# Matmuls whose result nobody reads, placed ahead of TensorE's waits in a hybrid mixer and expert trunk

## The chip, the cores and the metric

The kernel runs on one core of one Trainium2 chip. A core has five engines that run their own instruction streams and meet at semaphores: TensorE (PE in the rows; PEld is its weight load), VectorE (DVE), ScalarE (ACT), GpSimd (POOL) and SyncE (SP), which here issues all transfers. TensorE reads SBUF and writes PSUM, which has eight banks of 512 float32 columns on 128 partitions. Its clock has two levels, 2.4 GHz and 1.2 GHz; the profile lists what share of full speed was granted in each stretch (1.00 or 0.50).

The metric is the device time of one execution in microseconds (us), taken as the median of several runs.

## The reference, cut to what matters

Two pre-norm layers work on 256 positions of 1024 channels, in float32. Each has an RMS norm, four mixers that read the same normed input (short convolution, state space, gated MLP, pooling), sigmoid gates, an output projection, a second RMS norm and a channel mixer: dense in layer 0, top 2 of 8 experts in layer 1.

```python
for layer in range(DEPTH):
    h = rmsnorm(x, norm1_g[layer])
    proj = h @ w_in[layer]
    ...
    y_b = mamba2_mixer(z, xbc, dt_raw, ...)      # ends in an RMS norm over 4 groups
    ...
    x = x + merged.astype(x.dtype) @ w_out[layer]
    h2 = rmsnorm(x, norm2_g[layer])
    if layer % 2 == 0:
        f = swiglu(h2, ffn_wg[idx], ffn_wu[idx], ffn_wd[idx])
    else:
        f = moe_ffn(h2, router_w[idx], moe_wg[idx], moe_wu[idx], moe_wd[idx])
    x = x + f
return rmsnorm(x, final_g)
```

## The kernel before

**Arithmetic.** Every large product is made of three fast matmuls: each operand is split into a rounded part (`hi`) and the rest (`lo`), and hi·hi, hi·lo and lo·hi are added up in PSUM (`product`, for 256 columns each; the experts use 512 columns). ScalarE makes `weight_hi` (L367, in the experts L386) and VectorE makes `weight_lo` (L634, L667) from each weight unit of 1 MB that SyncE has loaded; a ring of three units stands between them and TensorE.

**Order.** All engines follow an order written out by hand. In each layer `norm_sums` comes first, then `PLAN`, a list of stages with so many weight units behind each, then the rest of the units. The last stages of `PLAN` are the norm of the state-space branch: `y_sq` (VectorE multiplies and squares, GpSimd adds pairs of squares, L1178), `y_sum` (TensorE sums the squares over channels by matmuls with one column of ones), one weight unit, `y_spread` (TensorE spreads the reciprocal roots over the partitions).

**The norms.** `norm_sums(n)` runs for n = 0 (first norm of layer 0, at the start), n = 1 (second norm of layer 0, inside the last output unit) and n = 2 (first norm of layer 1). It waits for the added squares (POOL L1119) and for the squares of the last channels (DVE L641), sums them into one column, waits for a diagonal matrix of the reciprocal roots (ACT L374, then DVE L646 and L648), and spreads it with one matmul of 256 columns. VectorE then writes h (L658) and `h_lo` (L637), ScalarE `h_hi` (L377), in pairs of channel blocks; TensorE goes on with the dense channel mixer (n = 1), or with the stage `dt_row`, full float32 matmuls over h that wait pair by pair (n = 2).

**Entry to the experts.** Transposes of x and the router's matmuls come in turns with the last output units. VectorE then picks the top two (L935 to L947, `sel_done`); TensorE makes two small matmuls that give each token its place; VectorE turns them into the selection matrix (L954 to L960, `pick_done`); `first_gather` selects the tokens of the first expert block by 32 matmuls of 128 columns; ScalarE and VectorE split the result (L516, L982), and the expert's weight products begin with `up`.

The matmuls all go through one helper, so nearly all of them have the line L1211. The tile `ones_r` holds ones, rounded for the fast matmul; before, the state-space stage `seg` reads it.

Of the kernel before, what the change touches and what calls it, by code (L numbers as in the profile page):

```python
# [100 lines left out]
def trunk(nc, x_in, par_in, con_in, fin_in, mix_w, ff_w, moe_w, out):  # L101
# [4 lines left out]
    with ctx:  # L106
# [36 lines left out]
        def bank(b, n=1):  # L143
            return PS[:, b:b + n, :].rearrange("p b n -> p (b n)")

        def tiles(ap, n=SEQ):
            return ap.rearrange("p (t n) -> p t n", n=n)
# [1061 lines left out]
        def _(pe):  # L1209
            def mm(o, a, b_, start, stop, **k):  # L1210
                return nc.tensor.matmul(o, a, b_, start=start, stop=stop, skip_group_check=True, **k)  # L1211

            def product(o, slot, blk, a_hi, a_lo, start, stop):

                w = slice(blk * P, (blk + 1) * P)
                mm(o, hi[:, slot, w], a_hi, start, False)
                mm(o, hi[:, slot, w], a_lo, False, False)
                return mm(o, lo[:, slot, w], a_hi, False, stop)
# [15 lines left out]
            def norm_sums(n):  # L1234

                for k in (0, 1, KT - 2, KT - 1):
                    if k == 0:
                        pe.wait_ge(S["sq_added"], n + 1)  # L1240
                    elif k == KT - 2:
                        pe.wait_ge(S["sq_done"], PAIRS * (n + 1))
                    for t in range(TT):
                        last = mm(bank(4 + t)[:, 0:1], sq[:, k, t * P:(t + 1) * P], C_("ones", 0, 1), k == 0, k == KT - 1)
                last.then_inc(S["norm_sum"], 1)
                pe.wait_ge(S["diag_done"], n + 1)
                mm(bank(7)[:, 0:SEQ], C_("ones"), diag, True, True).then_inc(S["rstd_ps"], 1)

            def early_unit(layer, u):

# [92 lines left out]
            def stage(name, layer):  # L1343
# [16 lines left out]
                elif kind == "xs_T":  # L1360

                    pe.wait_ge(S["conv_done"], XBC_BLOCKS * layer + 8)
                    pe.wait_ge(S["a_sc"], layer + 1)
                    for t in range(TT):
                        for c in range(8):
                            last = nc.tensor.transpose(bank(6 - 2 * t + c // 4)[:, (c % 4) * P:(c % 4 + 1) * P],
                                                       proj[:, XBC + c, t * P:(t + 1) * P], C_("ident"))
                        last.then_inc(S["xs_T"], 1)
                elif kind == "mean":
                    pe.wait_ge(S["gelu_done"], 2 * layer + 1)  # L1370
                    pe.wait_ge(S["xdt_done"], TT * (layer + 1))
                    for k in range(4):
                        last = mm(bank(7)[:, 0:SEQ], C_("ones"), v_[:, k, :], k == 0, k == 3)
                    last.then_inc(S["mean_sum"], 1)
                elif kind == "var":
                    pe.wait_ge(S["dev_sq"], layer + 1)
                    for t in range(TT):
                        for k in range(4):
                            last = mm(bank(7)[:, t:t + 1], v_sq[:, k, t * P:(t + 1) * P], C_("ones", 0, 1), k == 0, k == 3)
                    last.then_inc(S["var_sum"], 1)  # L1380
                elif kind == "ln":
                    pe.wait_ge(S["v_diag"], layer + 1)
                    mm(bank(7)[:, 0:SEQ], C_("ones"), v_diag, True, True).then_inc(S["v_rstd"], 1)
                elif kind == "v_T":
                    pe.wait_ge(S["v_norm"], layer + 1)
                    for t in range(TT):
                        for n in range(4):
                            last = nc.tensor.transpose(bank(4 + t)[:, n * P:(n + 1) * P], v_[:, n, t * P:(t + 1) * P], C_("ident"))
                    last.then_inc(S["v_T"], 1)
                elif kind == "spatial":  # L1390
                    pe.wait_ge(S["v_T_sb"], layer + 1)
                    pe.wait_ge(S["ws_masked"], layer + 1)
                    for n in range(4):
                        for t in range(TT):
                            at = (n % 2) * SEQ + t * P
                            last = mm(bank(6 + n // 2)[:, at:at + P], vT[:, t, n * P:(n + 1) * P], P_("ws", n * P, P), True, True)
                    last.then_inc(S["s_done"], 1)
                elif kind == "pool_out":
                    pe.wait_ge(S["pooled"], 4 * (layer + 1))
                    for n in range(4):  # L1400
                        last = mm(bank(4 + n // 2)[:, (n % 2) * SEQ:(n % 2 + 1) * SEQ], P_("pool_map", n * P, P), pooled[:, n, :], True, True)
                    last.then_inc(S["pool_out"], 1)
                elif kind == "cb":
                    pe.wait_ge(S["conv_done"], XBC_BLOCKS * (layer + 1))
                    if g == 0:
                        pe.wait_ge(S["yc_f"], layer + 1)
                    else:
                        pe.wait_ge(S["cb_done"], GROUPS * layer + 2)
                    for n in (2 * g, 2 * g + 1):
                        b_t, c_t = proj[:, XBC + 8 + n, :], proj[:, XBC + 12 + n, :]  # L1410
                        mm(bank(6 + n % 2)[:, 0:SEQ], b_t[:, 0:P], c_t, True, True)
                        mm(bank(6 + n % 2)[:, SEQ:SEQ + P], b_t[:, P:], c_t[:, P:], True, True).then_inc(S["cb_ps"], 1)
                elif kind == "seg":
                    pe.wait_ge(S["seg_in"], GROUPS * layer + g + 1)
                    pe.wait_ge(S["yd_f"], layer + 1)
                    pe.wait_ge(S["cb_done"], GROUPS * (layer + 1))

                    for n in range(2):
                        for part in range(2):
                            mm(bank(4 + n), after_r[:], flat(seg_in0[part][:, 2 * n:2 * n + 2, :]), part == 0, False)  # L1420
                        for part in range(2):
                            mm(tiles(bank(4 + n))[:, :, P:], ones_r[:], seg_in1[part][:, 2 * n:2 * n + 2, :], False, part == 1)
                    for part in range(2):
                        last = mm(bank(6), after_r[:], flat(seg_in1[part]), part == 0, part == 1)
                    last.then_inc(S["seg_done"], 1)
                elif kind == "y":
                    pe.wait_ge(S["score_done"], GROUPS * layer + g + 1)
                    if layer or g:
                        pe.wait_ge(S["y_done"], GROUPS * layer + g)
                    for n in range(4):  # L1430
                        head = 4 * g + n
                        o = bank(7)[HEAD_DIM * (n % 2):HEAD_DIM * (n % 2 + 1), (n // 2) * SEQ:(n // 2 + 1) * SEQ]
                        heads = slice(head * HEAD_DIM, (head + 1) * HEAD_DIM)
                        mm(o, xdt[:, 0, heads], dec0[:, n, :], True, False)
                        last = mm(o[:, P:], xdt[:, 1, heads], dec1[:, n, :], False, True)
                    last.then_inc(S["y_ps"], 1)
                elif kind == "y_sum":
                    pe.wait_ge(S["yb_sq_added"], layer + 1)
                    for n in range(GROUPS):
                        for t in range(TT):  # L1440
                            last = mm(bank(4)[:, TT * n + t:TT * n + t + 1], y_sq[:, 2 * n, t * P:(t + 1) * P], C_("ones", 0, 1), True, True)
                    last.then_inc(S["yb_sum"], 1)
                elif kind == "y_spread":
                    pe.wait_ge(S["yb_diag"], layer + 1)
                    for n in range(2):
                        last = mm(bank(4 + n), C_("ones"), scr[:, 512 * n:512 * n + 512], True, True)
                    last.then_inc(S["yb_rstd"], 1)
# [47 lines left out]

            pe.wait_ge(S["sel_done"], 1)
            chosen = route[:, 3 * TT * EXPERTS:4 * TT * EXPERTS]
            mm(bank(0)[:, 64:64 + TT * EXPERTS], C_("upto"), chosen, True, True)  # L1500
            mm(bank(0)[:, 64 + TT * EXPERTS:64 + 2 * TT * EXPERTS], C_("ones"), chosen, True, True).then_inc(S["pos_ps"], 1)

            def split_e_is(v, item):
                pe.wait_ge(lo_done, RING + MOE_U + v + item * ITEM_UNITS + 1)
# [234 lines left out]
```

## Time and profile before

| | us |
|---|---|
| median of 3 runs | 1993.43 (1992.45 to 1993.79) |
| the profiled execution: its time | 1993.0 |
| its span, first to last instruction | 1991.2 |
| PE busy / weight loads busy | 1921.5 (96%) / 1723.1 (87%) |
| VectorE / ScalarE / GpSimd busy | 1486.3 (75%) / 1172.5 (59%) / 288.7 (14%) |
| mean granted TensorE clock | 0.983 |

A row of the timeline gives start, duration, engine, line, operation, what is written from what, shape, and in brackets the idle time of the engine before it with the one that ended it. One float32 matmul leaves two records, so a count of x16 is eight matmuls. A matmul's duration holds its passage through the array; what one costs in a stream is the distance between two starts.

### The profile page before, as it was taken

To read this page: it belongs to the slowest core of one execution; us is meant where nothing else is said; L and a number is where in the kernel's file an instruction comes from. 1 tells how busy PE (TensorE), PEld (TensorE's weight loads), DVE (VectorE), ACT (ScalarE), POOL (GpSimd) and SP (SyncE) were. 2 spreads that over 40 slices of the span, in tenths; PEclk is the share of its full clock that TensorE was granted. 3 is DMA by queue.
4 is the path that set the end of the run, shared out by engine and by line. 5 is a ranking of instruction groups with operands and counts; after the bars stand their busy time and mean duration, and the time that the engine had idled before them with its cause. 6 is when DMAs were issued, how large, how long until landed. Compare 5 with 4: busy or idle time off the path is not lost.

```text
span 1991.2 us, 30489 instructions
## 1 busy us (share of the span) xinstructions
PE 1921.5 (96%) x11938; PEld 1723.1 (87%) x11938; DVE 1486.3 (75%) x1306; ACT 1172.5 (59%) x929; POOL 288.7 (14%) x247
## 2 busy tenths in 40 slices
PE   7999999899989999999999999999999999999997
PEld 6999998899989999989888888888888888888885
DVE  5775566754556765566698898988989889898896
ACT  4545453433335544534577777777777777777775
POOL 1047750000000156830120000000000000000000
PEclk9999999999989999989899999999999999999998
DMA  5444443455444444445489999999999999999893
GB/s 218 170 170 150 163 154 131 147 189 188 174 163 137 160 148 174 144 148 206 186 327 366 343 356 356 360 353 344 357 344 357 367 344 356 355 360 364 336 355 151
DMA packets 70203, 506.23 MB, mean 254 GB/s; under 512 B 7792, under 2 KB 8048, under 8 KB 9072
## 3 DMA queue, kind: packets, MB, share of 16 engines
q1 hardware_dynamic: 70128, 505.15, 68.1%
q8 instruction: 57, 0.93, 0.2%
q14 instruction: 18, 0.15, 0.0%
HBM read 504.07 MB, written 1.05 MB: 254 GB/s over the span
## 4 chain that ended last, share of the span: by engine, by line
PE 75%; DVE 9%; ACT 6%; issue 5%; POOL 4%; DMA 0%; SPq 0%; DVEq 0%; ACTq 0%; POOLq 0%
PE psum L1211 74%; ACT weight_hi L367 3%; DVE weight_lo L634 2%; DVE scr L772 2%; DVE weight_lo L667 1%; POOL pool_tmp L1156 1%; PE psum L1581 1%; ACT weight_hi L386 1%; POOL proj L1158 1%; ACT proj L438 1%; DVE scr L767 1%; POOL proj_r L1172 1%; POOL proj L1151 1%; POOL proj L1178 0%; DMA weight_raw<-mix_w 0%
## 5 line engine op out<-in xcount | busy, mean ns | idle before, releaser
L1211 PE MATMUL psum<-weight_hi,y_hi 128*128 128x512 f32 x1344 | 532.8, 396 | 7.5 <-DVE weight_lo L667 5.3
L634 DVE TENSOR_TENSOR weight_lo<-weight_raw,weight_hi 128x2048 fp32r<-128x2048 f32 x141 | 329.4, 2337 | 263.1 <-ACT weight_hi L367 262.3
L1211 PE MATMUL psum<-weight_hi,y_lo 128*128 128x512 f32 x1344 | 525.4, 391 | 0.0
L1211 PE MATMUL psum<-weight_lo,y_hi 128*128 128x512 f32 x1344 | 524.7, 390 | 0.0
L1211 PE MATMUL psum<-h_hi,weight_hi 128*128 128x256 f32 x1760 | 507.5, 288 | 10.1 <-DVE h_lo L637 6.0
L1211 PE MATMUL psum<-h_lo,weight_hi 128*128 128x256 f32 x1760 | 501.9, 285 | 0.0
L1211 PE MATMUL psum<-h_hi,weight_lo 128*128 128x256 f32 x1760 | 501.7, 285 | 0.0
L667 DVE TENSOR_TENSOR weight_lo<-weight_raw,weight_hi 128x2048 fp32r<-128x2048 f32 x165 | 377.7, 2293 | 83.3 <-ACT weight_hi L386 82.0
L386 ACT ACTIVATE weight_hi<-proj 128x2048 fp32r<-128x2048 f32 x169 | 323.8, 1921 | 128.2 <-PE psum L1211 128.2
L667 DVE TENSOR_TENSOR weight_lo<-proj,weight_hi 128x2048 fp32r<-128x2048 f32 x169 | 385.1, 2290 | 15.0 <-ACT weight_hi L386 13.3
L367 ACT ACTIVATE weight_hi<-weight_raw 128x2048 fp32r<-128x2048 f32 x141 | 268.8, 1906 | 147.1 <-PE psum L1211 144.6
L1211 PEld LDWEIGHTS psum<-h_hi,weight_hi 128*128 128x128 f32 x1760 | 341.8, 194 | 14.9 <-issue 7.1
L1211 PEld LDWEIGHTS psum<-h_lo,weight_hi 128*128 128x128 f32 x1760 | 341.8, 194 | 0.9 <-issue 0.5
L1211 PEld LDWEIGHTS psum<-h_hi,weight_lo 128*128 128x128 f32 x1760 | 341.6, 194 | 0.0
L386 ACT ACTIVATE weight_hi<-weight_raw 128x2048 fp32r<-128x2048 f32 x165 | 315.5, 1912 | 38.2 <-PE psum L1211 38.2
L1211 PEld LDWEIGHTS psum<-weight_hi,y_hi 128*128 128x128 f32 x1344 | 253.1, 188 | 64.8 <-DVE weight_lo L667 11.1
L1211 PEld LDWEIGHTS psum<-weight_hi,y_lo 128*128 128x128 f32 x1344 | 252.8, 188 | 54.1
L1211 PEld LDWEIGHTS psum<-weight_lo,y_hi 128*128 128x128 f32 x1344 | 253.2, 188 | 50.3
L1211 PE MATMUL psum<-y_hi,weight_hi 128*128 128x256 f32 x368 | 105.2, 286 | 2.1 <-DVE y_lo L637 2.1
L1211 PE MATMUL psum<-y_lo,weight_hi 128*128 128x256 f32 x368 | 104.9, 285 | 0.0
L1211 PE MATMUL psum<-y_hi,weight_lo 128*128 128x256 f32 x368 | 104.8, 285 | 0.0
L1211 PEld LDWEIGHTS psum<-y_hi,weight_hi 128*128 128x128 f32 x368 | 71.3, 194 | 2.8 <-issue 2.6
(256 smaller groups left out, 1726.8 us busy)
## 6 DMA issues: line engine op xcount, KB each, us to landing
proj<-moe_w SPq DMA_DIRECT2D x169, 1024.0 KB, 6.9
weight_raw<-moe_w SPq DMA_DIRECT2D x165, 1024.0 KB, 6.8
weight_raw<-mix_w SPq DMA_DIRECT2D x108, 1024.0 KB, 4.8
weight_raw<-ff_w SPq DMA_DIRECT2D x33, 1024.0 KB, 4.8
first_raw<-moe_w SPq DMA_DIRECT2D x2, 1024.0 KB, 5.9
par<-par_in SPq DMA_DIRECT2D x2, 768.0 KB, 9.7
x<-x_in SPq DMA_DIRECT2D x2, 512.0 KB, 4.6
out<-proj SPq DMA_DIRECT2D x2, 512.0 KB, 3.1
```

The costliest lines, as they stand in the source:

```text
L367: A(hi[:, slot, :], raw[:, slot, :], ACT.Copy).then_inc(hi_done, 1)
L386: A(hi[:, v % RING, :], raw_e(v), ACT.Copy).then_inc(hi_done, 1)
L438: A(proj[:, XBC + t, :], scr[:, (t % 4) * SEQ:(t % 4 + 1) * SEQ], ACT.Silu, bias=P_("ssm_b", t, 1)).then_inc(S["conv_done"], 1)
L634: V.tensor_tensor(lo[:, slot, :], raw[:, slot, :], hi[:, slot, :].bitcast(f32), ALU.subtract).then_inc(lo_done, 1)
L667: V.tensor_tensor(lo[:, v % RING, :], raw_e(v), hi[:, v % RING, :].bitcast(f32), ALU.subtract).then_inc(lo_done, 1)
L767: last = V.tensor_scalar(accs[:, t, :], raws[:, t, :], P_("ssm_w", 3 * XBC_BLOCKS + 2 * g + t, 1), None, ALU.mult)
L772: last = V.scalar_tensor_tensor(accs[:, t, s:], raws[:, t, :SEQ - s], P_("ssm_w", tap * XBC_BLOCKS + 2 * g + t, 1), accs[:, t, s:], ALU.mu ...
L1151: last = G.tensor_scalar(a_c[:, t, :], a_h[:, t, :], P_("sc_w", 2 * SC_BLOCKS + t, 1), None, ALU.mult)
L1156: last = G.tensor_scalar(sums_a[:, t, s:], a_h[:, t, :SEQ - s], P_("sc_w", tap * SC_BLOCKS + t, 1), None, ALU.mult)
L1158: link(G.tensor_tensor(a_c[:, :, s:], a_c[:, :, s:], sums_a[:, :, s:], ALU.add))
L1172: G.tensor_scalar(seg_in0[part][:, n, :], up_and_ones, da[:, 0, head].bitcast(f32), None, ALU.mult)
L1211: return nc.tensor.matmul(o, a, b_, start=start, stop=stop, skip_group_check=True, **k)
```

## The change

A function `idle(b, n)` issues n matmuls of the ones matrix with 512 columns of ones (the same 128 read four times) into bank b. Nothing reads the result and nothing is signalled. It is called six ways: 16 matmuls ahead of the wait of `y_sum` in both layers; in `norm_sums` for n = 1 and n = 2, 6 ahead of the first sum, 3 between the sums and the wait for the diagonal, 4 behind the spreading matmul; and at the entry to the experts 6 ahead of the wait for the selection and 5 behind the two place matmuls. All in all 69 matmuls are added; other engines' instructions and the transfers are the same, in the same order.

```diff
+            def idle(b, n):
+
+                wide = ones_r[:].rearrange("p (a n) -> p a n", a=1).broadcast_to([P, 4, P])
+                for _ in range(n):
+                    mm(tiles(bank(b), P), ones_r[:], wide, True, True)
+
...
+                if n:
+                    idle(6, 6)
                 for k in (0, 1, KT - 2, KT - 1):
                     if k == 0:
                         pe.wait_ge(S["sq_added"], n + 1)
...
                 last.then_inc(S["norm_sum"], 1)
+                if n:
+                    idle(6, 3)
                 pe.wait_ge(S["diag_done"], n + 1)
                 mm(bank(7)[:, 0:SEQ], C_("ones"), diag, True, True).then_inc(S["rstd_ps"], 1)
+                if n:
+                    idle(6, 4)
...
                 elif kind == "y_sum":
+                    idle(6, 16)
                     pe.wait_ge(S["yb_sq_added"], layer + 1)
...
+            idle(2, 6)
             pe.wait_ge(S["sel_done"], 1)
             chosen = route[:, 3 * TT * EXPERTS:4 * TT * EXPERTS]
             mm(bank(0)[:, 64:64 + TT * EXPERTS], C_("upto"), chosen, True, True)
             mm(bank(0)[:, 64 + TT * EXPERTS:64 + 2 * TT * EXPERTS], C_("ones"), chosen, True, True).then_inc(S["pos_ps"], 1)
+            idle(2, 5)
```

TensorE at `y_sum` of layer 0, before: the last product of a unit of early branches, the sums, the next unit.

```order
L1211 MATMUL psum<-y_lo,weight_hi 128x256
L1211 MATMUL psum<-y_hi,weight_lo 128x256
L1211 MATMUL psum<-con,proj 128x1 [waits yb_sq_added]
L1211 MATMUL psum<-con,proj 128x1 x7
L1211 MATMUL psum<-h_hi,weight_hi 128x256 [waits early_added,gate_done,lo_done]
```

The same place now:

```order
L1211 MATMUL psum<-y_lo,weight_hi 128x256
L1211 MATMUL psum<-y_hi,weight_lo 128x256
L1211 MATMUL psum<-ones_r 128x512 x16
L1211 MATMUL psum<-con,proj 128x1 [waits yb_sq_added]
L1211 MATMUL psum<-con,proj 128x1 x7
L1211 MATMUL psum<-h_hi,weight_hi 128x256 [waits early_added,gate_done,lo_done]
```

The sixteen stand ahead of the instruction that waits, so they can run while GpSimd adds the squares.

TensorE at the second norm of layer 0 (n = 1), before: the sums in two halves, the spreading matmul, the first product of the dense channel mixer.

```order
L1211 MATMUL psum<-con,proj 128x1 [waits sq_added]
L1211 MATMUL psum<-con,proj 128x1 x3
L1211 MATMUL psum<-con,proj 128x1 [waits sq_done]
L1211 MATMUL psum<-con,proj 128x1 x3
L1211 MATMUL psum<-scr,con 128x256 [waits diag_done]
L1211 MATMUL psum<-h_hi,weight_hi 128x256 [waits h_lo_done,lo_done]
```

The same place now; n = 2 is alike, with the `dt_row` matmuls in place of the last row:

```order
L1211 MATMUL psum<-ones_r 128x512 x6
L1211 MATMUL psum<-con,proj 128x1 [waits sq_added]
L1211 MATMUL psum<-con,proj 128x1 x3
L1211 MATMUL psum<-con,proj 128x1 [waits sq_done]
L1211 MATMUL psum<-con,proj 128x1 x3
L1211 MATMUL psum<-ones_r 128x512 x3
L1211 MATMUL psum<-scr,con 128x256 [waits diag_done]
L1211 MATMUL psum<-ones_r 128x512 x4
L1211 MATMUL psum<-h_hi,weight_hi 128x256 [waits h_lo_done,lo_done]
```

The first six stand ahead of all eight sums, also of the four that need only the added squares.

## Rows read from the trace of the kernel before

**Rows 1.** Stretches at half clock, and one in the experts: length, busy time, instructions, clock.
```profile
305.05:311.88 6.83, 6.83 (x34) 6.83 (x34) 3.74 (x4) 3.35 (x3) 0.00 (x0) 0.50 0.20 84
386.97:393.80 6.83, 4.63 (x21) 4.63 (x22) 6.31 (x13) 4.45 (x6) 0.00 (x0) 0.50 0.00 0
578.12:581.53 3.41, 3.41 (x18) 3.41 (x18) 2.91 (x3) 1.02 (x1) 0.00 (x0) 0.50 0.25 89
588.36:598.60 10.24, 8.10 (x24) 3.92 (x24) 6.37 (x15) 2.78 (x5) 1.00 (x3) 0.50 0.00 0
881.91:892.15 10.24, 8.83 (x41) 8.83 (x42) 5.75 (x6) 3.35 (x3) 1.36 (x1) 0.50 0.30 104
970.65:984.31 13.66, 12.38 (x45) 11.06 (x46) 9.03 (x25) 4.86 (x12) 0.00 (x0) 0.50 0.33 116
1025.00:1050.00 25.00, 25.00 (x116) 20.62 (x115) 23.10 (x15) 17.39 (x12) 0.00 (x0) 1.00 0.98 366
```
**Rows 2.** Timeline, PE, at the state-space sums of layer 0.
```profile
299.83 0.28 PE L1211 MATMUL psum<-y_lo,weight_hi 128*128 128x256 f32 x1
299.95 0.28 PE L1211 MATMUL psum<-y_hi,weight_lo 128*128 128x256 f32 x1
304.38 2.98 PE L1211 MATMUL psum<-con,proj 128*128 128x1 f32 x16 [4.14 <-POOL proj L1178]
307.22 0.56 PE L1211 MATMUL psum<-h_hi,weight_hi 128*128 128x256 f32 x1
307.58 0.41 PE L1211 MATMUL psum<-h_lo,weight_hi 128*128 128x256 f32 x1
307.80 0.41 PE L1211 MATMUL psum<-h_hi,weight_lo 128*128 128x256 f32 x1
```
**Rows 3.** Timeline, PE, at the same sums of layer 1.
```profile
883.32 3.58 PE L1211 MATMUL psum<-con,proj 128*128 128x1 f32 x16 [4.15 <-POOL proj L1178]
886.76 0.56 PE L1211 MATMUL psum<-h_hi,weight_hi 128*128 128x256 f32 x1
```
**Rows 4.** Timeline, PE, at the second norm of layer 0.
```profile
382.23 0.95 PE L1211 MATMUL psum<-con,proj 128*128 128x1 f32 x8
383.90 1.05 PE L1211 MATMUL psum<-con,proj 128*128 128x1 f32 x8 [0.72 <-DVE proj L641]
389.17 0.55 PE L1211 MATMUL psum<-h_hi,weight_hi 128*128 128x256 f32 x1 [2.45 <-DVE h_lo L637]
```
**Rows 5.** Timeline, DVE, at that norm: the last two pairs of h_lo.
```profile
391.11 1.47 DVE L637 TENSOR_TENSOR h_lo<-proj,h_hi 128x512 fp32r<-128x512 f32 x2
```
**Rows 6.** Timeline, PE, a pause in the gated MLP, layer 0 and layer 1.
```profile
132.24 0.70 PE L1211 MATMUL psum<-tmp,con 128*128 128x256 f32 x2 [2.95 <-DVE tmp L798]
708.47 1.22 PE L1211 MATMUL psum<-tmp,con 128*128 128x256 f32 x2 [2.95 <-DVE tmp L798]
```
**Rows 7.** Timeline, PE, at the first norm of layer 1.
```profile
587.32 2.66 PE L1211 MATMUL psum<-con,proj 128*128 128x1 f32 x16 [1.96 <-POOL proj L1119]
591.15 1.22 PE L1211 MATMUL psum<-scr,con 128*128 128x256 f32 x2 [1.17 <-DVE scr L648]
593.34 6.21 PE L1211 MATMUL psum<-proj,par 128*16 128x256 f32 x16 [0.97 <-DVE proj L658]
```
**Rows 8.** Timeline, PE, at the entry to the experts.
```profile
969.09 0.62 PE L1211 MATMUL psum<-par,con 128*128 128x16 f32 x4 [1.66 <-DVE par L947]
971.20 3.67 PE L1211 MATMUL psum<-y_hi,yb_hi 128*128 128x128 f32 x16 [1.49 <-ACT yb_hi L588]
979.02 0.77 PE L1211 MATMUL psum<-weight_hi,y_hi 128*128 128x512 f32 x1 [0.74 <-issue]
984.28 0.41 PE L1211 MATMUL psum<-weight_hi,y_hi 128*128 128x512 f32 x1
987.06 0.39 PE L1211 MATMUL psum<-weight_hi,y_hi 128*128 128x512 f32 x1
```
**Rows 9.** Timeline, DVE, there: the low part of the fourth weight unit.
```profile
986.51 2.29 DVE L667 TENSOR_TENSOR weight_lo<-first_raw,weight_hi 128x2048 fp32r<-128x2048 f32 x1 [0.67 <-ACT weight_hi L386]
```

## The prediction

> **What bounds the kernel now.** I read the table of busy shares first: TensorE is busy 96% of the span, so time is to be won only where it waits or runs slowly. The mean granted clock, 0.983, says that some 34 us of the span ran at half clock; cutting the span at the changes of the clock [rows 1] finds them: besides the start and the end, which this change leaves alone, six stretches stand there (a seventh lies behind a pause of the gated MLP in layer 1 [rows 6]). Five of the six begin at a place that the change touches. The sixth, at 578.12, follows a wait in the last dense step, which stays. Then the timeline of TensorE around each.
>
> What the rows say of the clock: it fell after stretches in which TensorE had little to do, and came back after dense products. Little to do is not waiting alone: in 305.05 to 311.88 TensorE counts as busy throughout [rows 1], over two microseconds of it with 16 records of a single column [rows 2], and the half clock stayed. And the same stretch can go either way: the pause of 2.95 us in the gated MLP left the clock full in layer 0 (the next two records take 0.70 us together) and at half in layer 1 (1.22 us) [rows 6]. So I can't say of a shortened pause that it keeps the clock; I give it a chance.
>
> The Trainium skill says why ("TensorE: Matmul & The Clock Gate", Part 1): the clock is judged in windows that run free of the program, so the same code may meet them at another place. The trace agrees in that one pair. By that rule the gain differs from run to run by a few microseconds, and a median of runs lies near the mean over such chances; none of the terms below needs it.
>
> **Prices.** A product matmul of 256 columns comes every 0.12 us at full clock (299.83, 299.95) and every 0.22 us at half (307.58, 307.80; more exactly 0.213, half the columns' rate) [rows 2]. So each microsecond of products at half clock costs 0.44 us. One of 512 columns: twelve starts from 984.28 to 987.06, 0.232 us each at full; twelve from 979.02 to 984.28, 0.438 at half [rows 8]. The added matmuls have that shape; nothing shows their weights (ones, every time) to be dearer or cheaper, so I bound one between 0.213 and 0.25 us and take 0.23. Single-column records: 8 in 0.95 us at full [rows 4], 16 in 3.58 at half [rows 3]; 16 at full are then 1.9.
>
> **State-space sums (16 added, twice).** 16 x 0.23 = 3.7 us, from about 300.1 to 303.8, against a wait that ends at 304.38 [rows 2]: hidden with 0.6 us to spare, so nothing is late. Behind them little work is left only for 0.6 us of waiting and 1.9 us of single columns, 2.5 us instead of more than 6. If the clock holds, layer 0 gains 2.98 - 1.9 = 1.1 us on the sums and (311.88 - 307.22) x 0.44 = 2.05 us on the products, 3.1 us. Layer 1: 3.58 - 1.9 = 1.7, and (892.15 - 886.76) x 0.44 = 2.4, 4.1 us [rows 1, 3]. Both places together: 7.2 us as the upper end; the lower is about -0.5 (nothing held, and the fall moved a little). A thin stretch of 2.5 us is shorter than the 2.95 us pause that went both ways; somewhat over half the cases should hold, and those that fall should fall for a shorter time. I take two thirds: 4.8 us. A whole weight unit of 48 products (5.8 us at full clock) stands between the sums and the spreading that needs ScalarE's roots and VectorE's diagonal, so nothing of that chain becomes late, and the gain goes through.
>
> **Second norm of layer 0 (6, 3, 4).** Here the first six are too many. TensorE is done with the products when the sums begin at 382.23; four of the eight sums then ran without waiting, and the other four waited until 383.90 [rows 4]. Six fills take 1.4 us, the first four sums end at about 384.6, so the second four start 0.7 us later than before, and roots, diagonal, spreading and h with them: +0.7 us. The 3 fills (0.7 us) and the 4 (0.9 us) fit into their waits, the second of which is 2.45 us. What a held clock could give back is 4.6 us of products at 0.44 [rows 1], 2.0 us, but VectorE delivers the last h_lo at 392.58 [rows 5], and the first unit needs it; behind that only 0.8 us can be won. Between +0.7 (clock falls as before) and -0.1; I take +0.3 slower.
>
> **First norm of layer 1 (6, 3, 4).** Here the six fit (1.4 us in a wait of 1.96), the three fit (0.7 in 1.17), the four just fit at full clock (0.92 in 0.97) and not at half (1.75: +0.8). If the clock holds: sums 2.66 to 1.9, spreading 1.22 to 0.70, and `dt_row`, 16 records in 6.21 us [rows 7], would be paced by VectorE's h (about 4.5 us for four pairs) instead: 0.75 + 0.5 + 1.8 = 3.0 us faster. Thin work remains from about 586.7 to 589.2, 2.5 us again, and is thin afterwards too. Between 3.0 faster and 0.8 slower; I take 1.0 faster.
>
> **Entry to the experts (6, 5).** 1.4 us into a wait of 1.66, and 1.15 into one of 1.49 [rows 8]: hidden. With the clock held, the 32 gather records, which came every 0.23 us, come every 0.12; the second 16 need VectorE's low parts, so I count 2.5 us, not 3.5. Then the chain ScalarE, VectorE (high and low part, some 2.4 us) must pass before `up` starts, at 976.5 instead of 979.02, and it leaves TensorE 1.5 us without work; whether the clock holds through that is open. If it does, the products until 984.31 cost 2.4 us less. Against that stands VectorE, which made the fourth unit's low part from 986.51 [rows 9] to 988.80, about 1 us before TensorE needed it; its chain moves up by 2.5 to 3 us only, so about 1.1 us of a 4.9 us lead is lost waiting: 3.8 us. Between 0 and 3.8; I take 3.0.
>
> The skill would make this term smaller ("TensorE: Matmul & The Clock Gate", Part 4: transposes are said not to count as work for the clock). Eight such matmuls stand right ahead of the fills. By it the clock could fall before the gather, and the term would be 1.5 instead of 3.0; no row here parts the two.
>
> **The sum.** -4.8 + 0.3 - 1.0 - 3.0 = -8.5 us on the profiled execution's own 1993.0 (span 1991.2 and 1.8 around it): 1984.5. The median shown is 0.4 higher: 1984.9 us.
>
> **Rivals.**
> 2. Everything holds: -7.2 - 0.1 - 3.0 - 3.8 = -14.1: 1979.3 us. For it: all added matmuls but the first six of n = 1 fit their waits. Against: five thin stretches of 2.5 us each. 12%.
> 3. The experts' stream takes back the entry's gain. For it: in 1025 to 1050 the transfers are busy 98% of the time at 366 GB/s, VectorE 92% [rows 1]. Against: TensorE has no pause in those rows, so it sets the pace. Then only the terms before: 1988.0 us. 10%.
> 4. Slower than before: the fills meet a clock that is already at half. The 16 then take 7.0 us against a wait of 4.14, +2.9 us in each layer, +0.7 and +0.8 at the norms, and 6 x 0.438 = 2.6 against 1.66, +1.0, at the experts: +8.3 us less what is gained later, about 1999. It decides where a fall comes less than 4 us ahead of the wait. Against: at 299.95 TensorE comes out of dense products 0.12 us apart, at full clock [rows 2], and in layer 1 the half clock begins only at 881.91 [rows 1]. 3%.
>
> The forecast itself has 55%, from 1981.5 to 1988.5. A difference of 0.2%, 4 us, is about what a measurement of this kernel tells from none. Faster by more (under 1989.4): nearly all of the forecast and of rival 2, two thirds of rival 3: 0.75. Within: most of rival 1, the rest of 3, the forecast's upper end: 0.22. Slower: 0.03. The range leaves out some of rival 1's end and a little of rival 2: 1979.0 to 1991.5.
>
> **What would show it.** Right: 16 records `psum<-ones_r` of 0.23 us ahead of the sums at about 300, the sums still at 304.4 in 2 us instead of 3 or 3.6, and the stretch at half clock gone or shorter in at least one layer; at the second norm of layer 0 the sums' second half 0.7 us later; gather records 0.12 us apart. Wrong: half clock at all five places with the lengths of before (rival 1); a wait of TensorE for weight_lo of over 3 us behind the entry (rival 3); fills 0.43 us apart (rival 4).

## The result

The changed kernel took 1976.09 us (median of 4 runs, 1975.54 to 1980.66) against 1993.61 us of the kernel before (4 runs, 1992.45 to 1994.39); the ratio is 0.9923, with a 95% interval of 0.9900 to 0.9947. The forecast was 1984.9 us, in a range of 1979.0 to 1991.5: so the result lies 2.9 us below the range. The sign and the mechanism were right, the size was half of what came. The profiled execution took 1975.86 us, 17.1 less than the profiled one of before (1993.0).

The page of the changed kernel: span, busy time of TensorE, and the granted clock in 40 slices, of which none but the last reads under 9.

```profile
span 1974.0 us, 30627 instructions
PE 1917.9 (97%) x12007; PEld 1717.3 (87%) x12007; DVE 1486.2 (75%) x1306; ACT 1172.2 (59%) x929; POOL 290.2 (15%) x247
PEclk9999999999999999999999999999999999999998
```

The span cut at the places of [rows 1]: start and end, length, busy time of PE, PEld, DVE, ACT and POOL, granted clock, share of the DMA engines, GB/s.

```profile
304.21:306.02 1.81, 1.81 (x16) 1.81 (x17) 0.66 (x2) 0.00 (x0) 0.00 (x0) 1.00 0.97 412
378.97:390.00 11.03, 8.49 (x52) 6.78 (x50) 7.75 (x17) 3.65 (x6) 0.00 (x0) 1.00 0.28 97
570.30:578.10 7.80, 5.74 (x48) 5.57 (x48) 6.05 (x8) 3.19 (x2) 0.00 (x0) 1.00 0.61 214
584.42:587.83 3.41, 3.41 (x10) 2.54 (x11) 1.32 (x5) 0.26 (x1) 0.32 (x1) 0.50 0.00 0
697.06:703.00 5.94, 2.99 (x24) 2.73 (x23) 3.64 (x5) 5.91 (x7) 5.27 (x6) 1.00 0.15 32
873.60:876.00 2.40, 2.22 (x19) 2.22 (x20) 0.83 (x2) 0.24 (x2) 0.12 (x1) 1.00 0.90 375
963.30:966.71 3.41, 3.41 (x9) 2.62 (x8) 3.31 (x8) 0.97 (x2) 0.00 (x0) 0.50 0.00 0
```

Besides the one at the end (10.2 us before, 10.6 now), two stretches at half clock are left in the span, 3.41 us each, where before seven stood with 58.0 us in all. And two places went back to full clock at which nothing was added: 570 to 578 (the wait in the last dense step) and 697 to 703 (the pause of the gated MLP in layer 1, which answers to [rows 6]).

TensorE's timeline at the state-space sums of layer 0, the answer to [rows 2], and of layer 1, to [rows 3]:

```profile
299.86 3.84 PE L1211 MATMUL psum<-ones_r 128*128 128x512 f32 x16
304.21 1.95 PE L1211 MATMUL psum<-con,proj 128*128 128x1 f32 x16 [0.51 <-POOL proj L1178]
306.02 0.37 PE L1211 MATMUL psum<-h_hi,weight_hi 128*128 128x256 f32 x1
306.22 0.28 PE L1211 MATMUL psum<-h_lo,weight_hi 128*128 128x256 f32 x1
...
869.43 3.84 PE L1211 MATMUL psum<-ones_r 128*128 128x512 f32 x16
873.78 1.95 PE L1211 MATMUL psum<-con,proj 128*128 128x1 f32 x16 [0.51 <-POOL proj L1178]
875.59 0.37 PE L1211 MATMUL psum<-h_hi,weight_hi 128*128 128x256 f32 x1
```

These rows show all that a held clock gives: the fills end 0.5 us before the sums may start, the sums take 1.95 us instead of 2.98 and 3.58, and the products follow.

At the second norm of layer 0 (answers to [rows 4]), at the first norm of layer 1 (to [rows 7]) and at the entry to the experts (to [rows 8]):

```profile
379.00 1.56 PE L1211 MATMUL psum<-ones_r 128*128 128x512 f32 x6
380.39 1.84 PE L1211 MATMUL psum<-con,proj 128*128 128x1 f32 x16
382.09 0.94 PE L1211 MATMUL psum<-ones_r 128*128 128x512 f32 x3
383.31 0.70 PE L1211 MATMUL psum<-scr,con 128*128 128x256 f32 x2 [0.28 <-DVE scr L648]
383.65 1.28 PE L1211 MATMUL psum<-ones_r 128*128 128x512 f32 x4
386.45 0.35 PE L1211 MATMUL psum<-h_hi,weight_hi 128*128 128x256 f32 x1 [1.51 <-DVE h_lo L637]
...
582.70 2.03 PE L1211 MATMUL psum<-con,proj 128*128 128x1 f32 x16 [0.93 <-POOL proj L1119]
584.59 1.63 PE L1211 MATMUL psum<-ones_r 128*128 128x512 f32 x3
586.02 1.10 PE L1211 MATMUL psum<-scr,con 128*128 128x256 f32 x2
586.56 1.89 PE L1211 MATMUL psum<-ones_r 128*128 128x512 f32 x4
588.37 2.92 PE L1211 MATMUL psum<-proj,par 128*16 128x256 f32 x12
...
957.66 2.00 PE L1211 MATMUL psum<-y_hi,yb_hi 128*128 128x128 f32 x16 [0.23 <-ACT yb_hi L588]
959.50 1.95 PE L1211 MATMUL psum<-y_hi,yb_lo 128*128 128x128 f32 x16
963.00 0.50 PE L1211 MATMUL psum<-weight_hi,y_hi 128*128 128x512 f32 x1 [1.54 <-issue]
```

**Where the 17.1 us came from.** TensorE's starts at eight marks, taken from both timelines: the last product ahead of the first sums, the first product behind the wait ahead of the output units, a product of the last dense step but one (564.15 before), the first product of layer 1, the last product ahead of its sums, the first of its output units, the first behind the first pause of the expert loop, the last matmul. The lengths between them, in us:

| section | before | changed | difference |
|---|---|---|---|
| state-space sums, layer 0 | 60.52 | 57.49 | -3.0 |
| output units, second norm, dense part | 203.67 | 203.42 | -0.3 |
| last dense step and first norm of layer 1 | 35.33 | 31.96 | -3.4 |
| mixers of layer 1 up to the sums | 279.42 | 276.70 | -2.7 |
| state-space sums, layer 1 | 61.45 | 57.49 | -4.0 |
| entry to the experts | 185.95 | 182.58 | -3.4 |
| expert loop and end | 856.66 | 856.43 | -0.2 |

The sections follow each other without a gap, and what lies ahead of the first mark differs by 0.2. Nothing was added in the fourth section, nor at the wait inside the third.

### The profile page after: what moved, and what is told of

Read it like the earlier page. It is cut to its first block, busy times and chain, and to the rows that moved or that the text cites. A ratio compares the mean times of both kernels' runs of the same rounds, so it can differ in the third digit from the quotient of the medians.

```text
span 1974.0 us, 30627 instructions
## 1 busy us (share of the span) xinstructions
PE 1917.9 (97%) x12007; PEld 1717.3 (87%) x12007; DVE 1486.2 (75%) x1306; ACT 1172.2 (59%) x929; POOL 290.2 (15%) x247
## 4 chain that ended last, share of the span: by engine, by line
PE 74%; DVE 9%; ACT 6%; POOL 5%; issue 5%; DMA 0%; SPq 0%; DVEq 0%; ACTq 0%; POOLq 0%
PE psum L1211 72%; ACT weight_hi L367 3%; DVE weight_lo L634 2%; DVE scr L772 2%; DVE weight_lo L667 1%; POOL proj_r L1172 1%; POOL pool_tmp L1156 1%; PE psum L1596 1%; ACT weight_hi L386 1%; POOL proj_r L1173 1%; POOL proj L1158 1%; ACT proj L438 1%; DVE scr L767 1%; POOL proj L1151 1%; POOL proj L1178 0%
## 5 line engine op out<-in xcount | busy, mean ns | idle before, releaser
L1211 PE MATMUL psum<-weight_hi,y_hi 128*128 128x512 f32 x1344 | 532.1, 396 | 8.3 <-DVE weight_lo L667 5.3
L1211 PE MATMUL psum<-weight_hi,y_lo 128*128 128x512 f32 x1344 | 525.2, 391 | 0.0
L1211 PE MATMUL psum<-weight_lo,y_hi 128*128 128x512 f32 x1344 | 524.4, 390 | 0.0
L1211 PE MATMUL psum<-h_hi,weight_hi 128*128 128x256 f32 x1760 | 503.3, 286 | 9.8 <-DVE h_lo L637 5.8
L1211 PE MATMUL psum<-h_lo,weight_hi 128*128 128x256 f32 x1760 | 497.9, 283 | 0.0
L1211 PE MATMUL psum<-h_hi,weight_lo 128*128 128x256 f32 x1760 | 497.9, 283 | 0.0
L1211 PEld LDWEIGHTS psum<-h_hi,weight_hi 128*128 128x128 f32 x1760 | 337.4, 192 | 15.0 <-issue 6.2
L1211 PEld LDWEIGHTS psum<-h_lo,weight_hi 128*128 128x128 f32 x1760 | 337.6, 192 | 0.8 <-issue 0.5
L1211 PEld LDWEIGHTS psum<-h_hi,weight_lo 128*128 128x128 f32 x1760 | 337.5, 192 | 0.0
L1211 PEld LDWEIGHTS psum<-weight_hi,y_hi 128*128 128x128 f32 x1344 | 252.8, 188 | 65.3 <-DVE weight_lo L667 11.1
L1211 PEld LDWEIGHTS psum<-weight_hi,y_lo 128*128 128x128 f32 x1344 | 252.7, 188 | 53.9
L1211 PEld LDWEIGHTS psum<-weight_lo,y_hi 128*128 128x128 f32 x1344 | 252.9, 188 | 50.3
L1211 PE MATMUL psum<-y_hi,weight_hi 128*128 128x256 f32 x368 | 104.5, 284 | 2.1 <-DVE y_lo L637 2.1
L1211 PE MATMUL psum<-y_lo,weight_hi 128*128 128x256 f32 x368 | 104.1, 283 | 0.0
L1211 PE MATMUL psum<-y_hi,weight_lo 128*128 128x256 f32 x368 | 104.1, 283 | 0.0
L527 ACT ACTIVATE y_hi<-psum 128x512 fp32r<-128x512 f32 x56 | 33.6, 600 | 66.4 <-PE psum L1596 66.4
```

The lines of the kernel that those rows point to most:

```text
L527: A(flat(hT_hi), bank(6), ACT.Copy).then_inc(S["hT_hi_done"], 1)
```

## The experiments

Each session ran on one chip, with the kernel before beside it; the sessions (experiment 1; experiments 2 and 3; experiments 4 and 5) had three different chips, on which the kernel before had means of 1992.4, 1992.0 and 1992.0 us. Besides the times I use the sections of the table, because they tell a place from its neighbours. Each trace is of one execution, and only the changed kernel has two of them.

**1. The start delayed, without and with the change.** The same work, meant to come 1.4 and 2.7 us later.

```diff
                         dve.wait_ge(x_loaded[q // 2], 16)
+                        if q == 2:
+                            for _ in range(2):        # 4 in b_d4 and a_d4
+                                link(V.tensor_tensor(flat(sq[:, 4:6, :]), flat(x[:, 4:6, :]), flat(x[:, 4:6, :]), ALU.mult))
                         squares(q)
```

Expected of b_d2: 

> The kernel before, with two more squares of the same 512 columns in VectorE's queue at the very start, so that all that follows comes about 1.4 us later. Theory A (the chip judges TensorE's activity at times that keep their place against the start of the program, so a given pause always meets them alike): the time is not simply 1.4 us longer; the six half-clock stretches change in number or length, two of the places the change leaves alone (the pause of the gated MLP in layer 1, the wait in the last dense step) may change side, and repeated runs agree within 1 to 2 us. Time between 1990 and 1998. Theory B (the times of judging are free against the program, luck differs from run to run): the repeated runs of this kernel scatter by 3 us and more. Theory C (place plays no part, the length of a pause decides): six stretches as before, time 1995.0 within 0.5.

Expected of b_d4: 

> The same with four more squares, all that follows about 2.7 us later. Theory A: again another set of half-clock stretches, time between 1990 and 1999, runs within 1 to 2 us of each other. Theory B: scatter of 3 us and more. Theory C: 1996.3, six stretches as before.

Expected of a_d2: 

> The changed kernel with the same start delay of about 1.4 us. Theory A: the thin stretches of 2.5 us that held now partly fall; time 1977 to 1986 where no luck were 1977.5; the runs agree within 2 us. Theory C (the added matmuls are enough wherever the stretch lies, the state-space sums and the norms hold always): 1977.5 within 1, the state-space sums' clock 1.00 in both layers.

Expected of a_d4: 

> The changed kernel with the start delay of about 2.7 us. Theory A: 1978 to 1988, another set of stretches at half clock than in the run without delay; at least one of the two state-space sums falls in this run or in that with 1.4 us. Theory C: 1978.8 within 1.

Measured: b_d2 1994.57 us (1990.19 to 1995.48, 10 runs, ratio 1.0007, interval 0.9997 to 1.0016), b_d4 1995.70 (1989.48 to 1996.45, 10 runs, 1.0009, 0.9998 to 1.0020), a_d2 1979.22 (1977.16 to 1981.22, 4 runs, 0.9935, 0.9918 to 0.9952), a_d4 1978.66 (1977.94 to 1986.40, 5 runs, 0.9939, 0.9918 to 0.9960). Beside them the kernel before, unchanged, ran 20 times between 1989.39 and 1994.57. The delay came through in part only. TensorE's first matmul began 1.5 and 2.8 us later in b_d2 and b_d4 (11.34 and 12.71 against 9.87), but its first product only 0.4 and 2.35 us later (23.64 and 25.58 against 23.23), because a wait behind the first sums became shorter; b_d2 shows the same seven stretches as before, 0.3 us later. So these runs say little about what a shift does. The repeated runs say more, and they are for theory B and against A: one and the same program scatters by 4 to 8.5 us. The medians of b_d2 and b_d4 come near those of theory C (1995.0 and 1996.3); the traces speak against it. The pause of the gated MLP, this time in layer 0, in the trace of b_d4, where L1211 has become L1214 (in [rows 6] it kept full clock there, 0.70 us), and in layer 1 in that of the changed kernel:

```profile
134.55 1.22 PE L1214 MATMUL psum<-tmp,con 128*128 128x256 f32 x2 [2.95 <-DVE tmp L798]
```
```profile
701.61 0.70 PE L1211 MATMUL psum<-tmp,con 128*128 128x256 f32 x2 [2.95 <-DVE tmp L798]
```

The same pause of 2.95 us, in the same code, at half clock and at full. The section of the state-space sums took 57.5 us without a fall in the changed kernel, and 58.99 with one in layer 1 of a_d4, so theory C falls too.

**2. One place at a time.**

```diff
 o_sums:  keeps   idle(6, 16)                        (the other calls removed)
 o_norms: keeps   idle(6, 6), idle(6, 3), idle(6, 4)
 o_exp:   keeps   idle(2, 6), idle(2, 5)
```

Expected of o_sums: 

> Only the 16 added matmuls ahead of the state-space sums, in both layers; none at the norms and the experts. Theory A (each place is worth what its own half-clock stretch cost, and places add up): both stretches at 305 and 882 gone in most runs, 3.1 and 4.0 us less at them, median 6 to 7 us under the kernel before; stretches at 387, 588 and 970 as before. Theory B (the gain at these places is only two thirds of that, as predicted, and the rest of the measured gain was luck at untouched places): 4 to 5 us under.

Expected of o_norms: 

> Only the 6, 3 and 4 added matmuls at the second norm of layer 0 and the first norm of layer 1. Theory A: the second norm of layer 0 0.5 us later at the sums and paid back by the clock, net 0 to 0.3 us gained; the first norm of layer 1 gains 2 to 2.5 us; together 2 to 3 us under the kernel before. Theory B (predicted sizes): 0.7 us under, no change that can be told.

Expected of o_exp: 

> Only the 6 and 5 added matmuls at the entry to the experts. Theory A: gather records 0.12 us apart, up starts about 2 us earlier after the router than before, 3.4 us under the kernel before, other places untouched. Theory B (the transfers or VectorE take it back in the expert stream): under 1 us, with a wait of TensorE for weight_lo behind the entry.

Measured: o_sums 1986.30 us (8 runs, ratio 0.9968, interval 0.9957 to 0.9979), o_norms 1989.14 (10 runs, 0.9984, 0.9975 to 0.9994), o_exp 1988.56 (10 runs, 0.9983, 0.9969 to 0.9997). In means over the runs, against a mean of 1992.0 of the kernel before (29 runs beside them, 1984.93 to 1994.59): 6.3, 3.5 and 4.3 us faster. The three add up to 14.1, and the changed kernel's mean over its ten runs (4 and, below, 6) is 1978.4, 13.6 us under that. Each of these differences is uncertain by about 1 us, so no interaction is needed, and a small one isn't excluded.

The profiled execution of o_sums had bad luck, which is instructive. Its timeline at the sums of layer 0, and its stretches at half clock in the two layers:

```profile
302.72 3.84 PE L1211 MATMUL psum<-ones_r 128*128 128x512 f32 x16
307.07 2.01 PE L1211 MATMUL psum<-con,proj 128*128 128x1 f32 x16 [0.51 <-POOL proj L1178]
```
```profile
308.80:312.20 3.40, 3.40 (x17) 3.40 (x18) 2.42 (x3) 3.07 (x3) 0.00 (x0) 0.50 0.06 24
882.30:885.70 3.40, 3.40 (x17) 3.40 (x17) 2.73 (x3) 3.35 (x3) 0.00 (x0) 0.50 0.01 2
```

The sums ran at full clock, and it fell behind them, for 3.4 us instead of 6.8 and 10.2 [rows 1]. Sections: 59.00 and 58.97, that is 1.5 us worse than held and still 1.5 and 2.5 better than in the profile before. Fills that do not hold the clock keep half of their worth or more. (Layer 1 was an unlucky draw in the profile before: its section without fills was 61.4 in two of five traces and 60.5 to 60.6 in three.)

In o_exp the entry section is 182.60, as in the changed kernel (without fills 185.4 to 186.1 in seven traces). In o_norms the last dense step fell as before, and the section with the first norm took 32.45 against 35.33: 2.9 us by the norm's fills alone. In o_sums and o_exp, without these fills, it took 32.52: the last dense step kept its clock (1.1 us), and the fall at the norm lasted 6.8 us instead of 10.2 (1.7 us), so luck there is worth almost as much. More traces part the two. From the first sum of this norm to the first product of layer 1, seven without these fills (before, b_d2, b_d4, o_sums, o_exp, sum8, sum28) took 10.5 to 12.2 us, 11.7 in the mean, and six with them (the changed kernel twice, a_d2, a_d4, o_norms, best) 9.3 to 10.8, 9.9 in the mean: the fills are worth 1.8 us there.

**3. Columns or occupancy.** The changed kernel with every added matmul made thin.

```diff
-                    mm(tiles(bank(b), P), ones_r[:], wide, True, True)
+                    mm(bank(b)[:, 0:1], C_("ones"), C_("ones", 0, 1), True, True)
```

Expected: 

> The changed kernel with each added matmul made into a float32 matmul of one column (two records, about as long on TensorE, 0.23 us, but hardly any columns). 
Measured: 1991.78 us (10 runs, ratio 1.0002, interval 0.9990 to 1.0013). TensorE's timeline at the sums of layer 0, and the stretch behind:

```profile
302.14 3.63 PE L1211 MATMUL psum<-con 128*128 128x1 f32 x32
306.46 3.45 PE L1211 MATMUL psum<-con,proj 128*128 128x1 f32 x16 [0.69 <-POOL proj L1178]
309.77 0.56 PE L1211 MATMUL psum<-h_hi,weight_hi 128*128 128x256 f32 x1
```
```profile
306.60:313.50 6.90, 6.90 (x33) 6.90 (x34) 3.40 (x5) 3.35 (x3) 0.00 (x0) 0.51 0.26 109
```

TensorE is busy but for 0.7 us, as with the wide fills, and the clock falls all the same, 0.2 us into the sums, with the loss of before (section 60.57). So being occupied was not enough. The thin fills differ from the wide ones in the number of columns and also in the type (plain float32 in two records, not the rounded float32 of the fast matmul); no run parts these two. The form of rival 1 by which ones times ones count for nothing falls by the changed kernel itself: its fills are of ones too, and they work.

**4. How many.** Only the sums, with 8 and with 28 in place of 16.

```diff
-                    idle(6, 16)
+                    idle(6, 8)         # sum28: idle(6, 28)
```

Expected of sum8: 

> Only the state-space sums, with 8 added matmuls in place of 16: 1.9 us of 4.3 filled, thin work of 4.4 us left behind them. Theory A (what stays thin decides): the clock falls in nearly every execution, but later, so that fewer products meet it; 2 to 4 us under the kernel before where the 16 gave 6. Rival (any break of the pause is enough): 6 us under, as with 16.

Expected of sum28: 

> Only the state-space sums, with 28 added matmuls: 6.5 us against a wait of 4.3, so the sums start 2.3 us late in each layer. Theory A (overshoot is paid in full, the clock is held always): from the sums' old place to the first output product 53.0 + 2.3 us in both layers and no half clock there; 1 to 2.5 us under the kernel before. Rival (the extra matmuls are dropped or overlapped): 6 us under or more.

Measured: sum8 1988.85 us (12 runs, ratio 0.9986, interval 0.9976 to 0.9996), sum28 1992.07 (12 runs, 1.0003, 0.9992 to 1.0014). The sums of layer 0, with 8 and with 28:

```profile
302.29 2.01 PE L1211 MATMUL psum<-ones_r 128*128 128x512 f32 x8
306.60 3.38 PE L1211 MATMUL psum<-con,proj 128*128 128x1 f32 x16 [2.29 <-POOL proj L1178]
309.84 0.56 PE L1211 MATMUL psum<-h_hi,weight_hi 128*128 128x256 f32 x1
```
```profile
302.22 6.57 PE L1211 MATMUL psum<-ones_r 128*128 128x512 f32 x28
308.62 1.84 PE L1211 MATMUL psum<-con,proj 128*128 128x1 f32 x16
310.32 0.36 PE L1211 MATMUL psum<-h_hi,weight_hi 128*128 128x256 f32 x1
```

With 8 the clock fell in both layers (sections 60.54 and 58.94). With 28 it held in both, at 59.43: the sums start 2.1 us late, and the section is 1.94 us longer than with 16 and a held clock, so the overshoot is paid nearly in full. The sections say 1 and 2 us gained against the profile before; the median says 0.3 us gained and the mean 0.5 us lost, where I expected a gain of 1 to 2.5. Its profile shows half clock at the gated MLP in both layers, at the last dense step and at both norms, but that is one execution of twelve, and one of the faster ones (1990.8); luck elsewhere should average out over twelve. In the three slowest runs (1996.35 to 1996.83) the mean granted clock was 0.983, as in the kernel before, so there the 28 matmuls were paid and the clock was not gained. At which place is not shown, and the missing gain stays open.

**5. The changed kernel once more, and a version with more fills.**

```diff
-                if n:
-                    idle(6, 6)
+                if n == 2:
+                    idle(6, 6)
...
                     elif k == KT - 2:
+                        if n == 1:
+                            idle(6, 3)
                         pe.wait_ge(S["sq_done"], PAIRS * (n + 1))
...
                 elif kind == "ln":
+                    idle(6, 11)
                     pe.wait_ge(S["v_diag"], layer + 1)
...
+                    idle(6, 8)
                     split_is(f0 + FF_UNITS - 1)
                     pe.wait_ge(S["hid_done"], 2 * FF_STEPS)
...
             first_gather()
+            idle(1, 6)
             pe.wait_ge(S["zeros_done"], 1)
...
             for n in range(2):
+                if n:
+                    idle(5, 14)
                 pe.wait_ge(S["ys_lo_done"], last_item + 2 + n)
```

Expected of after2: 

> The changed kernel once more, for more executions. Theory A (luck of place against the chip's judging, of the size of some us): a median of 1977 to 1979, above the first one of 1976.1, with a scatter from 1975 to 1982; state-space sums 53.0 or 54.5 us from the sums to the first output product. Theory B (the first median was typical): 1976 within 0.5.

Expected of best: 

> The changed kernel with the fills that its trace and the others ask for: the first six at the second norm of layer 0 become three between its two halves of sums; 11 more ahead of the wait for the gated MLP's diagonal (both layers), 8 ahead of the last dense step's wait, 6 between the gather and the experts' first product, 14 ahead of the last wait of the program. Theory A (each thin stretch costs by chance, whether the change touched it or not): no half clock at the gated MLP, at the last dense step, behind the gather and in the last 10 us; 2 to 4 us under the changed kernel, median 1973 to 1976, and a smaller scatter. Rival (further fills delay what they stand before): no faster than the changed kernel, or slower by up to 2 us.

Measured: after2 1980.69 us (6 runs, 1975.41 to 1981.55, ratio 0.9942, interval 0.9925 to 0.9959), best 1975.51 (6 runs, 1973.73 to 1978.19, ratio 0.9917, interval 0.9903 to 0.9932). The changed kernel's ten runs lie in two heaps, five at 1975.4 to 1976.3 and five at 1980.3 to 1981.6; the first median fell in the lower one, the second in the upper. The mean granted clock was 0.995 or 0.996 in every run of the lower heap and 0.991 to 0.993 in the upper: about 12 us more at half clock, and at 0.44 us for each of them that is the 5 us. Both profiles are of the lower heap, so which places make it is not shown. The profile of a_d4, at 1981.51 with 0.992, shows what such a run can look like: it has half clock at the second norm, 6.8 us of it at the first norm of layer 1, and 3.4 us each at the gated MLP, the sums of layer 1 and the wait of 1.74 us ahead of layer 1's output units.

The extra fills do what they should where they stand. The entry and the end of best:

```profile
966.11 1.61 PE L1211 MATMUL psum<-ones_r 128*128 128x512 f32 x6
967.82 0.47 PE L1211 MATMUL psum<-weight_hi,y_hi 128*128 128x512 f32 x1
968.12 0.39 PE L1211 MATMUL psum<-weight_lo,y_hi 128*128 128x512 f32 x1
...
1963.45 3.35 PE L1211 MATMUL psum<-ones_r 128*128 128x512 f32 x14
1967.44 0.50 PE L1211 MATMUL psum<-y_hi 128*128 128x512 f32 x1 [0.64 <-DVE y_lo L1085]
1967.78 0.39 PE L1211 MATMUL psum<-y_lo,y_hi 128*128 128x512 f32 x1
```

The entry section is 180.80 (1.8 less than the changed kernel), the last one 855.82 (0.6 less), and no stretch at half clock lies at the gated MLP, at the last dense step, behind the gather or ahead of the last matmul. In this profile (1978.19 us, the slowest of the six runs) the clock fell behind both state-space sums (59.00, 58.97) and at the first norm of layer 1, and also 1.6 us behind a wait of 1.74 us ahead of layer 0's output units that I had left alone; the second section took 204.37, 0.95 more than in the changed kernel. In the same session it is 5.2 us under the changed kernel by median and 3.7 by mean, with overlapping runs; that it is faster is likely, and by how much is open.

## Why the prediction was wrong

Point by point, by its own steps:

- **What bounds, and the prices: right, but for one reading.** The mean granted clock of 0.983 does not say that 34 us ran at half clock: half clock is half of full, so it says 68 us (58.0 in the seven stretches and 10.2 at the end), of which at most half was lost time. No term of the sum rests on it. A wide fill came every 0.230 us, single columns 16 in 1.95 (predicted 0.23 and 1.9); they fit their waits as worked out. That a thin stretch may go either way, and that single columns don't hold the clock, was right, as experiments 1 and 3 show.
- **State-space sums: full value right, share wrong.** Held, they gave 3.0 and 4.0 us (predicted 3.1 and 4.1). The share of two thirds was hardly more than the chance of holding ("somewhat over half"), as if a place that fell were worth almost nothing, though the same paragraph expected a shorter fall. With 16 fills the clock held in 7 of the 12 profiled places, and a fall cost 1.5 us, not 3 to 4. Against the profile before that makes 3.0 + 4.0 - 2 x 0.6 = 5.8; against the mean of the five traces without these fills (60.7 and 60.9) it makes 5.4, and o_sums measured 6.3. In the profiled execution both held: 7.0 against 4.8, 2.2 us of the miss.
- **Second norm of layer 0: about right.** The second half of the sums came 0.5 us late instead of 0.7, the end 0.3 faster instead of 0.3 slower; with a fall it was 0.3 slower (203.9 to 204.0 in a_d2, a_d4 and o_norms). Seven traces without fills there have 203.5 to 204.0 too, so nothing was gained or lost there that can be told.
- **First norm of layer 1: term too small.** I took 1.0 of a possible 3.0. In the changed kernel the norm gave 2.3, of the section's 3.4, although its clock did fall, for 3.4 us instead of 10.2: again a short fall costs little. 1.3 us of the miss. In the mean over the traces of experiment 2 the norm's fills give 1.8.
- **Entry to the experts: right.** 3.4 us against 3.0, and it went through the expert stream (856.3 to 856.7 us in all traces but that of best, with and without), so rival 3 falls. The first product of `up` came 2.5 us earlier, as worked out. The clock held through the gather and the wait behind it and fell 0.3 us after that product, so only 0.9 us came from the products. The upper end of 3.8 was too low: in best, where the clock held on, the entry gave 5.1, and the 1.1 us that I took off for VectorE's low parts was not lost.
- **Places without fills: the term that was missing.** I wrote that the sixth stretch "stays", since the change leaves its wait. The wait stayed and the half clock did not: 1.1 us there and 2.7 us at the gated MLP. I had seen in [rows 6] that the same pause goes both ways, and used it only as doubt about the new thin stretches, not for the old ones. In the profile of before, two of the three untouched places (both gated MLPs and the last dense step) had gone badly; another execution was likely to do better. This is 3.8 us of the miss. Luck fits it in size: the profiled execution of before lay 1.0 us above its kernel's mean and that of the changed kernel 2.5 us below its own, and the first median (17.5 us) too lay above the difference of means (13.6). But one draw is not all. Where no fill stood, the clock fell at the last dense step in 7 of 13 traces and at the gated MLP of layer 1 in 8 of 13. These two places cost 3.4 us in the mean in the three traces without any fill (before, b_d2, b_d4) and 0.7 us in the four with all of them (the changed kernel twice, a_d2, a_d4). Whether the change also bettered the odds of the places that it leaves alone is not shown; these traces are too few.

2.2 + 0.6 + 1.3 + 0.4 + 3.8 make 8.3 of the 8.6 us between the 8.5 that were forecast and the 17.1 that the profiles show. So two steps failed. The term for places without fills was put at nothing, and the share of the full value at the sums and at the first norm of layer 1 was set too low, because a fall that fills shorten to 3.4 us leaves half of the gain or more. Against the difference of means, 13.6, the forecast of 8.5 was still 5.1 too low: the parts alone measured 6.3, 3.5 and 4.3 against my 4.8, 0.7 and 3.0. The excess of the experts (1.3) is about the uncertainty of such a difference (1 us); that of the norms is more. The sections of the four touched places give 5.4 - 0.1 + 1.8 + 3.1 = 10.2 in the mean over the traces with and without their fills (sums, second norm, first norm of layer 1, entry). The other 3.4 us of the mean gain are of the size of what the two places without fills show, and stay open.

The Trainium skill ("TensorE: Matmul & The Clock Gate", Part 1) says the windows of judging run free of the program; experiment 1 agrees, by a scatter of 5 us in one program and by the pause at 132 and 134. The prediction added that a median of runs lies near the mean; here it did not, since the ten runs lie in two heaps (1975.4 to 1976.3, 1980.3 to 1981.6) with the mean of 1978.4 between them. By Part 4 of the same page of the Trainium skill, which says that transposes do not count as busy time in the same way, the clock could have fallen ahead of the gather; in the changed kernel it held from 587.83 to 963.30, over the transposes at 951 and 952, though no run isolates them.

## What to carry to other kernels

Where TensorE waits for some microseconds behind dense work, and half clock follows, wide matmuls that nobody reads can win back much of what that half clock costs (here 0.44 us for each microsecond of products), as long as they end before the wait does: what runs over is paid nearly in full (28 in place of 16: 1.94 us for each place). They don't hold the clock every time (7 of 12 places), but they shorten the fall. The waits left without fills go on to fall by chance, and a wait of 1.74 us was enough for it in best. And a profile of one execution shows one draw: before a stretch at half clock is counted as a cost that stays, or as a gain, look whether the same pause elsewhere in the trace went the other way.

## What the runs showed that I had not expected

- The kernel before scattered from 1984.93 to 1994.59 us over 29 runs; the first three had lain within 1.3 us.
- The length of a fall, not only whether it comes, is what fills shorten: 3.4 us where 6.8 and 10.2 stood.
- 32 single-column records in 3.63 us, back to back, did not keep the clock in the one trace that has them; 16 wide matmuls in 3.84 us did in 7 of 12 places.
